# Splitting the last feed-forward's first weight chunk during the output projection, and sharing one token tile's writes differently

## The chip, the cores and the metric

The kernel runs on one core of a Trainium2 chip. The metric is the device time of one execution in microseconds, as the median of several runs. Before the change it is 4000.79 us over 3 runs (3994.6, 4000.79 and 4008.6 us). Engines are named as the profile names them: PE is TensorE, DVE is VectorE, ACT is ScalarE, POOL is GpSimd, SP issues the DMAs.

## What is computed

The reference is a chain of three network blocks over 512 tokens and 1024 channels. Only the end of the third block matters here: a gated merge of two branches, an output projection, a layer norm, a gated feed-forward of 2816 hidden channels and a second layer norm, whose result is the output.

```python
def _layernorm(x, g, b):
    mu = jnp.mean(xf, axis=-1, keepdims=True)
    var = jnp.mean(jnp.square(xf - mu), axis=-1, keepdims=True)
    return ((xf - mu) * lax.rsqrt(var + LN_EPS) * g + b).astype(x.dtype)
...
        x = _layernorm(ALPHA * x + mixed @ w_out[layer], ln1_g[layer], ln1_b[layer])
        ffn = (jax.nn.silu(x @ w_ffn_gate[layer]) * (x @ w_ffn_up[layer])) @ w_ffn_down[layer]
        x = _layernorm(ALPHA * x + ffn, ln2_g[layer], ln2_b[layer])
```

## The kernel before

The program is a list of stages (blocks), one after the other; between two stages all engines meet at a barrier. Inside a stage each engine has its own instruction list, written out by hand, and the lists meet at semaphores. Activations lie with channels on the partitions: `G.x` ("residual") is 8 tiles of 128 channels by 512 tokens.

**Exact products.** A float32 product is made of three passes of a reduced format: each operand is split into a rounded "high" part and the "low" rest, and `exact_product` (L208 to L213) adds high*low, low*high and high*high. So every weight chunk (128 x 4096 numbers, 2 MB) that SP loads into one of two slots of `weight_ring` has to be split before TensorE can use it: one engine copies it into the high part, GpSimd subtracts that from the original for the low part. SP may load chunk n+2 when chunk n has been split (`feed`, L111).

**The merge stage** (`gated_merge`, L4740). GpSimd splits 40 units, a quarter of a chunk each, with a cast (L4036) and a subtraction (L4038). The last 8 units are the output projection. TensorE sums it into PSUM as four token tiles of 128 tokens (j = 0 to 3), in two halves of 512 channels (c = 0, 1), and for each tile it closes the sums and then, one tile behind, turns the normalised rows back (`rows_turned`, L262). After tile 2's turn it waits until tile 0's first half has been written, runs two matmuls of ones to keep busy (`keep_running`, L222) and turns tile 3.

**The layer norm of a token tile** goes round three engines. VectorE measures the two halves (BN_STATS, L271; their total, L273), adds the epsilon (L275), ScalarE takes the root (L287), VectorE inverts it (L277) and multiplies mean and inverse to an offset (L279: a SCALAR_TENSOR_TENSOR on 128 x 1 numbers with two inputs in SBUF). Then ScalarE normalises both halves (L290), TensorE turns them (L262), and the turned tiles, still in PSUM, are scaled and shifted into `G.x`: four instructions on ScalarE for the first 512 channels (`first_columns`, L298) and four on VectorE for the second 512 (`second_columns`, L306). Each engine does the writes of tile j-1 behind its work on tile j. ScalarE so writes tile 2's and tile 3's first halves one after the other at the end, and VectorE tile 2's second half and tile 3's.

**The last feed-forward** (`feed_forward`, called at L4933 as ffn4) starts behind the merge's barrier. Its first up-chunk is in the ring by then, unsplit. ScalarE rounds its first half in 8 pieces (L514), each in front of one tile of the input (L519), with the whole second half (L507) in between; GpSimd subtracts the pieces (L388) and then the second half (L377); VectorE makes the low part of the input (L617). TensorE first runs two matmuls of ones (L222), then the first half piece by piece (48 matmuls), then the second half when GpSimd is done with it. From there on each half is split while TensorE works on an earlier one. The stage ends with the same layer norm, whose writes are followed by eight stores to the output (L368), in order of tile and half.

## Time and profile before

| | us |
|---|---|
| median of 3 runs | 4000.79 |
| the profiled execution | 4000.84 |
| its span, first to last instruction | 3999.1 |
| PE busy | 3857.1 (96%) |
| DVE busy | 2271.8 (57%) |
| POOL busy | 1348.2 (34%) |
| ACT busy | 1339.6 (33%) |

The span is what the rows are timed in: their times count from its start. The last feed-forward runs from about 3620 us to the end, the merge's output projection from about 3574 to 3620 us. A busy share is an average over all stages: it does not say which engine the others wait for in the few microseconds between two stages.

### The profile page before, as it was taken

The numbers are of one execution on the slowest core, as the hardware profiler recorded it, in microseconds if no ns is written. First come the engines' busy times: TensorE is split into PE (matmuls) and PEld (weight loads), VectorE is DVE, ScalarE is ACT, GpSimd is POOL, SyncE is SP. The second block draws the span as 40 slices with busy tenths as digits, with TensorE's granted clock in tenths as the row PEclk, the third lists the DMA queues.
The fourth block names the chain that finished last, engine by engine and source line by source line (L and its number), as shares of the span: only waits on it lengthen the run. The fifth ranks groups of instructions, "written<-read, shape, count | busy, mean of one in ns | idle before, by whom it ended". The sixth has DMA issues, their size and how long they took to land. (4 is left out here: it accounts for less than half of the span.)

```text
span 3999.1 us, 63729 instructions
## 1 busy us (share of the span) xinstructions
PE 3857.1 (96%) x26795; PEld 3057.6 (76%) x26795; DVE 2271.8 (57%) x3322; ACT 1339.6 (33%) x2176; POOL 1348.2 (34%) x554
## 2 busy tenths in 40 slices
PE   8999999999999999988889999999999999999999
PEld 6866788867678887577776788777777777887887
DVE  5756567477667765577884776465551616332023
ACT  3356333243223333444443433322223111204223
POOL 1011444443233441000001444355454343664443
PEclk9999999999999999999999999999999999999999
DMA  5311222232122223431112222222121111322222
GB/s 179 129 62 36 92 105 84 105 113 106 63 80 88 105 88 114 174 138 50 50 41 88 84 95 95 91 85 84 64 84 68 71 67 53 127 84 91 99 93 76
DMA packets 46655, 359.87 MB, mean 90 GB/s; under 512 B 4387, under 2 KB 8867, under 8 KB 27084
## 3 DMA queue, kind: packets, MB, share of 16 engines
q1 hardware_dynamic: 46412, 356.35, 24.7%
q8 instruction: 187, 3.06, 0.3%
q14 instruction: 56, 0.46, 0.0%
HBM read 333.79 MB, written 22.28 MB: 89 GB/s over the span
## 5 line engine op out<-in xcount | busy, mean ns | idle before, releaser
L377 POOL TENSOR_TENSOR ffn_weights_low<-weight_ring,ffn_weights_high 128x2048 fp32r<-128x2048 f32 x128 | 591.4, 4620 | 776.4 <-ACT ffn_weights_high L507 775.6
L211 PE MATMUL banks<-ffn_in_high,ffn_weights_low 128*128 128x512 f32 x1888 | 738.5, 391 | 9.9 <-POOL ffn_weights_low L377 9.0
L212 PE MATMUL banks<-ffn_in_low,ffn_weights_high 128*128 128x512 f32 x1888 | 735.7, 390 | 0.0
L213 PE MATMUL banks<-ffn_in_high,ffn_weights_high 128*128 128x512 f32 x1888 | 735.6, 390 | 0.0
L507 ACT ACTIVATE ffn_weights_high<-weight_ring 128x2048 fp32r<-128x2048 f32 x128 | 245.2, 1915 | 559.1 <-PE banks L213 559.1
L211 PEld LDWEIGHTS banks<-ffn_in_high,ffn_weights_low 128*128 128x128 f32 x1888 | 355.1, 188 | 90.5 <-POOL ffn_weights_low L377 12.0
L212 PEld LDWEIGHTS banks<-ffn_in_low,ffn_weights_high 128*128 128x128 f32 x1888 | 355.1, 188 | 74.1 <-issue 0.7
L213 PEld LDWEIGHTS banks<-ffn_in_high,ffn_weights_high 128*128 128x128 f32 x1888 | 355.1, 188 | 74.0
L652 DVE SCALAR_TENSOR_TENSOR ffn_gate<-ffn_up,columns_sb,ffn_gate 128x511 f32<-128x511 f32 (+1 forms) x132 | 272.9, 2068 | 160.8 <-ACT ffn_value L542 160.8
L4038 POOL TENSOR_TENSOR third_weights_low<-weight_ring,third_weights_high 128x1024 fp32r<-128x1024 f32 x143 | 357.2, 2498 | 11.5
L4036 POOL CAST third_weights_high<-weight_ring 128x1024 fp32r<-128x1024 f32 x143 | 157.3, 1100 | 513.9 <-PE banks L213 485.1
L211 PE MATMUL banks<-third_x_high,third_weights_low 128*128 128x512 f32 x736 | 299.9, 407 | 2.7 <-DVE merge_gate L4898 0.9
L213 PE MATMUL banks<-third_x_high,third_weights_high 128*128 128x512 f32 x736 | 288.3, 392 | 0.0
L212 PE MATMUL banks<-third_x_low,third_weights_high 128*128 128x512 f32 x736 | 287.7, 391 | 0.0
L673 DVE TENSOR_TENSOR ffn_in_low<-ffn_hidden,ffn_in_high 128x512 fp32r<-128x512 f32 x80 | 165.8, 2120 | 141.0 <-ACT ffn_in_high L556 141.0
L3798 POOL TENSOR_TENSOR rwout_weights_low<-weight_ring,rwout_weights_high 128x1024 fp32r<-128x1024 f32 x8 | 18.6, 2380 | 606.7 <-ACT rwout_weights_high L3850 606.7
L211 PEld LDWEIGHTS banks<-third_x_high,third_weights_low 128*128 128x128 f32 x736 | 139.3, 189 | 32.6 <-issue 3.1
L213 PEld LDWEIGHTS banks<-third_x_high,third_weights_high 128*128 128x128 f32 x736 | 138.7, 188 | 30.0
L212 PEld LDWEIGHTS banks<-third_x_low,third_weights_high 128*128 128x128 f32 x736 | 139.4, 189 | 26.7 <-issue 1.0
L545 ACT ACTIVATE ffn_gate<-ffn_gate 128x512 f32<-128x512 f32 x66 | 41.8, 633 | 319.6 <-DVE ffn_gate L652 319.6
L211 PE MATMUL banks<-first_in_high,first_weights_low 128*128 128x512 f32 x336 | 140.0, 417 | 3.5 <-DVE first_in_low L1226 3.5
L665 DVE TENSOR_TENSOR ffn_hidden<-ffn_gate,banks 128x512 f32 (+1 forms) x22 | 15.1, 688 | 217.0 <-ACT ffn_gate L547 217.0
(703 smaller groups left out, 7878.9 us busy)
## 6 DMA issues: line engine op xcount, KB each, us to landing
weight_ring<-weights SPq DMA_DIRECT2D x143, 2048.0 KB, 7.7
scan_in<-rwkv_operands SPq DMA_DIRECT2D x7, 1280.0 KB, 5.7
rwkv_operands<-rwin_staged SPq DMA_DIRECT2D x23, 256.0 KB, 2.2
scan_in<-rwkv_operands SPq DMA_DIRECT2D x8, 512.0 KB, 3.9
bias_tiles<-bias_rows SPq DMA_DIRECT2D x8, 448.0 KB, 8.9
residual<-x SPq DMA_DIRECT2D x4, 512.0 KB, 6.3
hyena_u_x_T<-decay SPq DMA_DIRECT2D x2, 1024.0 KB, 8.1
rwkv_residual<-residual SPq DMA_DIRECT2D x1, 2048.0 KB, 7.2
```

The costliest lines, as they stand in the source:

```text
L211: pe.matmul(out, w[1], x[0], start=start, stop=False, skip_group_check=True)
L212: pe.matmul(out, w[0], x[1], start=False, stop=False, skip_group_check=True)
L213: return pe.matmul(out, w[0], x[0], start=False, stop=stop, skip_group_check=True)
L377: pool.tensor_tensor(parts[1], landed, parts[0].bitcast(F32), ALU.subtract).then_inc(S["split"], 1)
L507: act.activation(parts[0], landed, ACT.Copy).then_inc(S["rounded"], 1)
L545: act.activation(gc[:, h, :], gc[:, h, :], act_func).then_inc(S["activated"], 1)
L652: ins = dve.scalar_tensor_tensor(out=buf[:, h, to], in0=up_scaled[:, h, q, of], scalar=G.col(taps, 8 * t + 4 * q + tap), in1=buf[:, h, to] ...
L665: dve.tensor_tensor(gT[:, t, :], gc[:, h, :], G.banks[:, b + 1, :], ALU.mult).then_inc(S["hidden"], 1)
L673: dve.tensor_tensor(parts[1], gT[:, t, :], parts[0].bitcast(F32), ALU.subtract).then_inc(S["tile_split"], 1)
L3798: pool.tensor_tensor(w_parts[1][:, k, :], landed(k), w_parts[0][:, k, :].bitcast(F32), ALU.subtract).then_inc(S["split"], 1)
L4036: pool.tensor_copy(parts[0], landed).then_inc(S["rounded"], 1)
L4038: pool.tensor_tensor(parts[1], landed, parts[0].bitcast(F32), ALU.subtract).then_inc(S["split"], 1)
```

## The change

The first chunk of ffn4's weights is split before its stage begins. In the merge stage, behind its last input tiles and ahead of the layer norm, ScalarE waits for that chunk to land and copies both halves into new buffers (`ffn4_ahead_high`); GpSimd, behind its 40 units, subtracts both halves into `ffn4_ahead_low`. These buffers lie over the memory of `mlstm_out_T`, which nobody reads any more once the branch's units are used (`used` at 24). ffn4 takes the buffers as its weight buffers and leaves its own out; it raises the semaphores for the pieces at once, and ScalarE there only rounds the input. In all feed-forwards the weight buffers are allocated ahead of the others, so their tiles have other addresses.

The second part: in both layer norms VectorE writes the first half of token tile 2 (`spare_columns`) between tile 2's and tile 3's second halves, and ScalarE no longer does. The stores wait for the new semaphore there.

```diff
@@ -232,7 +232,7 @@
-ROWS = ("row_sum", "row_stats", "row_mean", "row_var", "row_root", "row_inverse", "row_offset", "row_normed", "row_turned", "row_first", "row_second")
+ROWS = ("row_sum", "row_stats", "row_mean", "row_var", "row_root", "row_inverse", "row_offset", "row_normed", "row_turned", "row_first", "row_spare", "row_second")
@@ -299,15 +299,28 @@
+def column_tile(dve, G, name, c, q, j):
...
+    k = JT * c + q
+    return dve.tensor_scalar(G.x[:, k, j * P:(j + 1) * P], row_bank(G, c, j)[:, q * P:(q + 1) * P],
+                             G.col(name + "_g", k), G.col(name + "_b", k), ALU.mult, ALU.add)
...
+def spare_columns(dve, G, R, name, j):
...
+    dve.wait_ge(R["row_turned"], 2 * j + 1)
+    for q in range(JT):
+        column_tile(dve, G, name, 0, q, j).then_inc(R["row_spare"], 1)
...
     for q in range(JT):
-        dve.tensor_scalar(G.x[:, JT + q, j * P:(j + 1) * P], row_bank(G, 1, j)[:, q * P:(q + 1) * P],
-                          G.col(name + "_g", JT + q), G.col(name + "_b", JT + q), ALU.mult, ALU.add).then_inc(R["row_second"], 1)
-def feed_forward(G, name, gain, taps, act_func, shift=0, keep=1.0, norm=None, root=False):
+        column_tile(dve, G, name, 1, q, j).then_inc(R["row_second"], 1)
+def feed_forward(G, name, gain, taps, act_func, shift=0, keep=1.0, norm=None, root=False, ahead=None):
@@ -323,6 +336,8 @@
                   "out_squared", "out_squares_added", "out_sums", "out_mean", "out_root", "out_inverse")
+        w_parts = [G.sb(name + "_weights_" + part, [P, 2, half], F32R, ctx=ctx) for part in ("high", "low")]
+        w_parts = ahead or w_parts
         stats = row_tiles(G, name, ctx) if norm else None
@@ -331,7 +346,6 @@
         vc = G.sb(name + "_value", [P, 2, SEQ], ctx=ctx)
-        w_parts = [G.sb(name + "_weights_" + part, [P, 2, half], F32R, ctx=ctx) for part in ("high", "low")]
         x_parts = [G.sb(name + "_in_" + part, [P, KT, SEQ], F32R, ctx=ctx) for part in ("high", "low")]
@@ -363,8 +377,13 @@
                 for j in range(JT):
-                    for c, columns in enumerate((S["row_first"], S["row_second"])):
-                        sp.wait_ge(columns, JT * (j + 1))
+                    for c in range(2):
+                        if c:
+                            sp.wait_ge(S["row_second"], JT * (j + 1))
+                        elif j == JT - 2:
+                            sp.wait_ge(S["row_spare"], JT)
+                        else:
+                            sp.wait_ge(S["row_first"], JT * min(j + 1, JT - 1))
                         sp.dma_start(G.aps["out"][c * JT * P:(c + 1) * JT * P, j * P:(j + 1) * P].rearrange("(k p) n -> p k n", p=P),
@@ -378,16 +397,21 @@
                 for h in range(2):
-                    if isinstance(i, int) and p == i == h == 0:
+                    if isinstance(i, int) and p == i == 0 and h <= (ahead is not None):
                         continue
...
-            landed, parts = landed_half(0, 0, True)
-            for k in range(KT):
-                pool.wait_ge(S["piece_high"], k + 1)
-                pool.tensor_tensor(parts[1][:, k, :], landed[:, k, :], parts[0][:, k, :].bitcast(F32), ALU.subtract).then_inc(S["piece_split"], 1)
-            pool.wait_ge(S["piece_split"], KT)
-            pool.sem_inc(S["split"], 1)
+            if ahead:
+                pool.sem_inc(S["rounded"], 1)
+                pool.sem_inc(S["piece_split"], KT)
+                pool.sem_inc(S["split"], 2)
+            else:
+                landed, parts = landed_half(0, 0, True)
+                for k in range(KT):
+                    pool.wait_ge(S["piece_high"], k + 1)
+                    pool.tensor_tensor(parts[1][:, k, :], landed[:, k, :], parts[0][:, k, :].bitcast(F32), ALU.subtract).then_inc(S["piece_split"], 1)
+                pool.wait_ge(S["piece_split"], KT)
+                pool.sem_inc(S["split"], 1)
             pairs_from_one(pool, UP_CHUNKS, chunk)
@@ -514,12 +538,13 @@
             for k in range(KT):
-                pieces((k,))
+                if not ahead:
+                    pieces((k,))
                 if gain is None:
...
                     act.activation(x_parts[0][:, k, :], G.x[:, k, :], ACT.Identity, scale=G.col(gain, k)).then_inc(S["x_high"], 1)
-                if k == KT // 2:
+                if k == KT // 2 and not ahead:
                     high(0, 0, 1, True)
@@ -595,7 +620,7 @@
                     rows_normed(act, G, S, stats, rows, j)
-                    if j:
+                    if 0 < j < JT - 1:
                         first_columns(act, G, S, norm, j - 1)
@@ -705,6 +730,7 @@
                         second_columns(dve, G, S, norm, j - 1)
+                spare_columns(dve, G, S, norm, JT - 2)
                 second_columns(dve, G, S, norm, JT - 1)
@@ -4739,7 +4765,7 @@
         S = stage(G, "merge", ctx, "gates_in", "restored", "rounded", "split", "used", "tile_high", "tile_split", "gate_done", "branch_done", "mixed", "kept",
-                  *ROWS)
+                  "next_rounded", "next_split", *ROWS)
@@ -4754,6 +4780,10 @@
+        def next_half(h):
...
+            return G.chunk(units // 4, KT)[:, :, h * 256:(h + 1) * 256], [w[:, h, :].rearrange("p (k n) -> p k n", k=KT) for w in T.next_weights]
@@ -4784,6 +4814,10 @@
                     split_unit(pool, S, column_unit(G, c, n % 4), [w.rearrange("p (k n) -> p k n", k=KT) for w in w_parts(n)], n)
+            for h in range(2):
+                landed, next_parts = next_half(h)
+                pool.wait_ge(S["next_rounded"], h + 1)
+                pool.tensor_tensor(next_parts[1], landed, next_parts[0].bitcast(F32), ALU.subtract).then_inc(S["next_split"], 1)
@@ -4872,9 +4906,14 @@
                 tile_high(tiles + k)
+            act.wait_ge(S["used"], unit_b)
+            G.arrived(act, units // 4 % 2, units // 8)
+            for h in range(2):
+                landed, next_parts = next_half(h)
+                act.activation(next_parts[0], landed, ACT.Copy).then_inc(S["next_rounded"], 1)
             for j in range(JT):
                 rows_normed(act, G, S, stats, rows, j)
-                if j:
+                if 0 < j < JT - 1:
                     first_columns(act, G, S, "ln1", j - 1)
@@ -4911,6 +4950,7 @@
                     second_columns(dve, G, S, "ln1", j - 1)
+            spare_columns(dve, G, S, "ln1", JT - 2)
             second_columns(dve, G, S, "ln1", JT - 1)
@@ -4919,6 +4959,7 @@
         T = Shared()
+        ahead = T.next_weights = G.over("ffn4_ahead_", [P, 2, CHUNK // 2])
         T.haT = G.sb("mlstm_out_T", [P, M_HEADS * MT_, SEQ], ctx=ctx)
@@ -4930,7 +4971,7 @@
             gated_merge(G, T)
-    feed_forward(G, "ffn4", None, None, ACT.Silu, keep=ALPHA, norm="ln2")
+    feed_forward(G, "ffn4", None, None, ACT.Silu, keep=ALPHA, norm="ln2", ahead=ahead)
```

GpSimd's list from the merge's last unit on, before:

```order
L4036 CAST third_x_high<-weight_ring 128x1024
L4038 TENSOR_TENSOR third_x_low<-weight_ring,third_x_high 128x1024
L4740 UNCONDITIONAL_BRANCH
L372 UNCONDITIONAL_BRANCH
L388 TENSOR_TENSOR ffn_weights_low<-weight_ring,ffn_weights_high 128x256 x8
L377 TENSOR_TENSOR ffn_weights_low<-weight_ring,ffn_weights_high 128x2048
```

And with the change (its lines are numbered some 25 to 40 higher; the unconditional branches are the ends of stages):

```order
L4062 CAST third_x_high<-weight_ring 128x1024
L4064 TENSOR_TENSOR third_x_low<-weight_ring,third_x_high 128x1024
L4820 TENSOR_TENSOR ffn_ahead_low<-weight_ring,ffn_ahead_high 128x2048 x2
L4766 UNCONDITIONAL_BRANCH
L391 UNCONDITIONAL_BRANCH
```

Two subtractions of 2048 columns now stand directly behind the last unit, in front of the barrier; eight pieces and one half are gone from behind it.

ScalarE's list from the last input tiles of the projection to the start of ffn4, before:

```order
L4856 ACTIVATE third_x_high<-normed 128x512 x4
L287 ACTIVATE merge_row_inverse<-merge_row_inverse 128x1
L290 ACTIVATE merge_gate<-banks,merge_row_offset,merge_row_inverse 128x512 x2
...
L298 ACTIVATE residual<-banks,columns_sb 128x128 x8
L4740 UNCONDITIONAL_BRANCH
L501 UNCONDITIONAL_BRANCH
L514 ACTIVATE ffn_weights_high<-weight_ring 128x256
L519 ACTIVATE ffn_in_high<-residual 128x512
```

With the change:

```order
L4890 ACTIVATE third_x_high<-normed 128x512 x4
L4913 ACTIVATE ffn_ahead_high<-weight_ring 128x2048 x2
L287 ACTIVATE merge_row_inverse<-merge_row_inverse 128x1
L290 ACTIVATE merge_gate<-banks,merge_row_offset,merge_row_inverse 128x512 x2
...
L298 ACTIVATE residual<-banks,columns_sb 128x128 x4
L4766 UNCONDITIONAL_BRANCH
L525 UNCONDITIONAL_BRANCH
L544 ACTIVATE ffn_in_high<-residual 128x512 x8
```

The two copies stand ahead of the first root; at the end four writes are left of eight, and ffn4 starts with the input tiles alone.

VectorE's list at the end of the merge, before:

```order
L279 SCALAR_TENSOR_TENSOR merge_row_offset<-merge_row_moments,merge_row_inverse 128x1
L306 TENSOR_SCALAR residual<-banks,columns_sb 128x128 x8
L4740 UNCONDITIONAL_BRANCH
L602 UNCONDITIONAL_BRANCH
L617 TENSOR_TENSOR ffn_in_low<-residual,ffn_in_high 128x512 x8
```

With the change:

```order
L279 SCALAR_TENSOR_TENSOR merge_row_offset<-merge_row_moments,merge_row_inverse 128x1
L305 TENSOR_SCALAR residual<-banks,columns_sb 128x128 x12
L4766 UNCONDITIONAL_BRANCH
L627 UNCONDITIONAL_BRANCH
L642 TENSOR_TENSOR ffn_in_low<-residual,ffn_in_high 128x512 x8
```

VectorE has twelve writes behind its last offset where it had eight; the same holds at the end of ffn4.

## Rows read from the trace of the kernel before

**Rows 1.** Timeline, TensorE: start, length, operation, count, idle time before and its releaser.

```profile
3606.00 1.33 PE L262 MATMUL banks<-constants_sb,merge_gate 128*128 128x128 f32 x8
...
3616.41 1.32 PE L262 MATMUL banks<-constants_sb,merge_gate 128*128 128x128 f32 x8 [0.28 <-ACT merge_gate L290]
3620.12 2.42 PE L222 MATMUL banks<-constants_sb 128*128 128x448 f32 x4 [2.39 <-PEq L4740]
3622.02 0.95 PE L211 MATMUL banks<-ffn_in_high,ffn_weights_low 128*128 128x512 f32 x1
...
3634.62 0.50 PE L211 MATMUL banks<-ffn_in_high,ffn_weights_low 128*128 128x512 f32 x1 [0.20 <-POOL ffn_weights_low L377]
```

**Rows 2.** Timeline, ScalarE, the merge's layer norm.

```profile
3605.17 1.45 ACT L290 ACTIVATE merge_gate<-banks,merge_row_offset,merge_row_inverse 128x512 f32<-128x512 f32 x2 [0.42 <-DVE merge_row_offset L279]
...
3616.92 2.90 ACT L298 ACTIVATE residual<-banks,columns_sb 128x128 f32<-128x128 f32 x8
```

**Rows 3.** Timeline, VectorE, the merge's layer norm and ffn4's first input tiles.

```profile
3601.43 0.70 DVE L271 BATCH_NORM_STATS2 merge_row_parts<-banks 128x6 f32<-128x512 f32 x1 [25.34 <-PE banks L213]
3603.38 0.70 DVE L271 BATCH_NORM_STATS2 merge_row_parts<-banks 128x6 f32<-128x512 f32 x1 [1.25 <-PE banks L213]
...
3604.98 0.16 DVE L279 SCALAR_TENSOR_TENSOR merge_row_offset<-merge_row_moments,merge_row_inverse 128x1 f32<-128x1 f32 x1
...
3607.79 1.36 DVE L306 TENSOR_SCALAR residual<-banks,columns_sb 128x128 f32<-128x128 f32 x4
3609.06 0.70 DVE L271 BATCH_NORM_STATS2 merge_row_parts<-banks 128x6 f32<-128x512 f32 x1
...
3615.46 1.36 DVE L306 TENSOR_SCALAR residual<-banks,columns_sb 128x128 f32<-128x128 f32 x4
...
3621.07 5.37 DVE L617 TENSOR_TENSOR ffn_in_low<-residual,ffn_in_high 128x512 fp32r<-128x512 f32 x5 [1.93 <-ACT ffn_in_high L519]
```

**Rows 4.** Timeline, GpSimd, around the barrier.

```profile
3599.24 2.40 POOL L4038 TENSOR_TENSOR third_x_low<-weight_ring,third_x_high 128x1024 fp32r<-128x1024 f32 x1
3620.59 5.30 POOL L388 TENSOR_TENSOR ffn_weights_low<-weight_ring,ffn_weights_high 128x256 fp32r<-128x256 f32 x5 [18.96 <-ACT ffn_weights_high L514]
...
3629.74 4.83 POOL L377 TENSOR_TENSOR ffn_weights_low<-weight_ring,ffn_weights_high 128x2048 fp32r<-128x2048 f32 x1 [0.18 <-POOL ffn_weights_low L388]
```

**Rows 5.** Timeline, VectorE and ScalarE, the last writes of the kernel.

```profile
3990.60 1.36 DVE L306 TENSOR_SCALAR residual<-banks,columns_sb 128x128 f32<-128x128 f32 x4
...
3992.06 2.90 ACT L298 ACTIVATE residual<-banks,columns_sb 128x128 f32<-128x128 f32 x8
```

**Rows 6.** Lines L507 and L377: duration in ns, least, median and most.

```profile
L507 ACT ACTIVATE ffn_weights_high<-weight_ring x128: 1891/1917/1922, 449.8 to 3964.9; 128x2048 fp32r<-128x2048 f32 x128
...
L377 POOL TENSOR_TENSOR ffn_weights_low<-weight_ring,ffn_weights_high x128: 4545/4605/5061, 455.4 to 3966.9; 128x2048 fp32r<-128x2048 f32 x128
```

**Rows 7.** Timeline, SP: the load of ffn4's first chunk.

```profile
3580.28 0.34 SPq L121 DMA_DIRECT2D weight_ring<-weights  x1
```

**Rows 8.** Windows: length, busy time by engine, granted clock, DMA share, GB/s.

```profile
3588.00:3590.00 2.00, 2.00 (x11) 1.65 (x10) 0.00 (x0) 0.00 (x0) 0.78 (x1) 1.00 0.00 0
```

**Rows 9.** Line L1506, a small VectorE operation elsewhere: duration in ns.

```profile
L1506 DVE TENSOR_TENSOR attn_stats<-attn_stats,branch_gates x48: 161/161/1640, 239.9 to 375.5; 128x2 f32<-128x2 f32 x48
```

**Rows 10.** Timeline, GpSimd and VectorE, at one of L1506's long ones.

```profile
243.03 2.37 POOL L1359 TENSOR_TENSOR first_weights_low<-weight_ring,first_weights_high 128x1024 fp32r<-128x1024 f32 x1 [8.39 <-ACT first_weights_high L1443]
...
243.79 1.63 DVE L1506 TENSOR_TENSOR attn_stats<-attn_stats,branch_gates 128x2 f32<-128x2 f32 x1
```

**Rows 11.** Windows, at the start of ffn4, columns as in rows 8.

```profile
3621.10:3624.40 3.30, 3.30 (x8) 2.03 (x7) 3.28 (x4) 3.30 (x9) 3.20 (x4) 0.50 0.00 0
```

**Rows 12.** Timeline, GpSimd and VectorE, VectorE operations with one tensor input.

```profile
2602.38 2.39 POOL L4038 TENSOR_TENSOR third_weights_low<-weight_ring,third_weights_high 128x1024 fp32r<-128x1024 f32 x1
...
2602.41 0.20 DVE L4337 TENSOR_SCALAR gate_small<-gate_small,normed 4x1 f32<-4x1 f32 x1
2602.64 2.20 DVE L4338 TENSOR_SCALAR residual<-residual,normed 4x128 f32<-4x128 f32 x1
```

## The prediction

> **What bounds the kernel now.** TensorE is busy 96% of the span (the table of the profile), so time can only come or go where it waits. I read the waits of the last 400 us first and found TensorE waiting in three places: at the end of the merge, at the start of ffn4 and at the very end. Then I read the timeline of each engine there. In the first place the path is a round of four engines. VectorE's offset (3604.98) releases ScalarE's pass (3605.17), and TensorE's turn of tile 0 starts 0.83 us behind that pass (3606.00) [rows 1, 2, 3]. The last turn ends at 3616.41 + 1.32 = 3617.73, and ScalarE's eight writes end last, at 3616.92 + 2.90 = 3619.82 [rows 1, 2]. Then comes the barrier; TensorE starts ffn4 at 3620.12, 0.30 later, and its first real matmul at 3622.02. Its second half starts at 3634.62, released by GpSimd, which ended at 3629.74 + 4.83 = 3634.57 [rows 1, 4]. At the end of the kernel ScalarE's eight writes (3992.06 + 2.90 = 3994.96) are what the last stores wait for [rows 5].
>
> **The added work.** ScalarE's two copies cost 1.92 us each [rows 6]. The chunk's load is issued at 3580.28 [rows 7], and by 3588 no transfer runs any more, while ScalarE does nothing [rows 8]. So the copies run at about 3588 to 3592, and the next thing ScalarE is wanted for is the first root, shortly before 3604.98. I cost them at nothing; this cover is some 12 us thick. If the chunk came later than about 3600, every us more would delay the first root.
>
> GpSimd's two subtractions are another matter. Its last unit ends at 3599.24 + 2.40 = 3601.64 [rows 4], and only then do they start: 4.61 us each [rows 6], so from about 3601.7 to 3606.3 and from 3606.3 to 3610.9. Nobody waits for their results before 3620. But they run beside the layer norm, during which GpSimd was idle before.
>
> What that does to VectorE is not in the rows of this stage, since there GpSimd was off. Elsewhere it is. L1506, a TENSOR_TENSOR on 128 x 2 numbers whose two inputs lie in SBUF, takes 0.161 us as a rule and up to 1.640 [rows 9]. The long one shown started at 243.79 while GpSimd ran from 243.03 to 245.40, and it ended at 245.42, just behind it [rows 10]. So a VectorE operation with two inputs in SBUF is held until GpSimd's operation is over, however small it is. In the norm's chain that is one operation, the offset L279, on 128 x 1 numbers with both inputs in SBUF. BN_STATS, from PSUM, is not held: it took 0.70 at 3601.43, when GpSimd still ran until 3601.64, and 0.70 at 3603.38, when it was idle [rows 3, 4]. The writes L306 read PSUM too. With the change the chain goes like this, each start worked out from the row named:
>
> Tile 0: the offset is issued at 3604.98 as before, in the middle of GpSimd's first subtraction, and ends at about 3606.35 instead of 3605.14 (+1.2). TensorE's turn of tile 0 starts at 3607.2 instead of 3606.00.
> Tile 1: VectorE needs two BN_STATS, of 0.70 each, and 0.90 more to the offset (3603.38 + 0.70 to 3604.98 [rows 3]): 3606.35 + 2.30 = 3608.65. There GpSimd's second subtraction holds it until 3610.95.
> From here nothing is held, and VectorE has no slack: writes of tile 0 in 1.27 (3607.79 to 3609.06 [rows 3]) to 3612.2, BN_STATS and the rest 2.30 + 0.16 to 3614.7, writes of tile 1 to 3615.9, tile 3's measuring to 3618.4. TensorE's sums are ready for these steps, by my placing: its last turn follows tile 3's offset and is over when VectorE comes to the writes that need it.
>
> **The moved writes.** VectorE now has twelve writes behind the last offset: 2 x 1.27 + 1.36 = 3.9 us, from 3618.4 to 3622.3; ScalarE, with four, is done before. The merge ends at 3622.3 instead of 3619.82: +2.5. Without any holding VectorE would start these writes at 3615.46 [rows 3] and end at 3619.36: -0.45. So the moved writes alone gain 0.45, and the holding costs about 2.95.
>
> **The start of ffn4.** ScalarE starts with the input tile instead of a weight piece, and VectorE's low parts no longer run against GpSimd: five of them took 5.37 us beside five pieces in 5.30 [rows 3, 4]. But TensorE's two matmuls of ones (2.42 [rows 1]) still come first. The first real matmul stood 1.90 behind the start of the stage; it can't come earlier than the ones allow, and the gain lies between 0 and 0.5. I take 0.2, nearer to the row. The wait for GpSimd at 3634.62 is gone: the row gives 0.20 of idle time ahead of a matmul of 0.50 [rows 1]; I take 0.35, between 0.2 and 0.5. What is late next there is TensorE itself, matmul behind matmul.
>
> **TensorE's clock.** It was granted half (1.2 GHz) in 3621.10 to 3624.40 [rows 11]; before that TensorE had been idle from 3617.73 to 3620.12. About 2.4 us of that stretch lay on real matmuls, which cost 1.2. With the change TensorE stalls at other points. If the clock doesn't fall, 1.2 are gained; if the whole stretch of 3.3 us falls on real matmuls, it costs 1.65, 0.45 more than now. I take no difference, since an idle time of some 2 us stays ahead of the barrier's end.
>
> **The end of the kernel.** GpSimd has nothing to do there. VectorE's twelve writes run from 3990.60 to 3994.5 instead of ScalarE's end at 3994.96, and the store of tile 2's first half waits for VectorE at 3990.60 + 2 x 1.27 + 0.1 = 3993.2 instead of ScalarE's fourth write at 3993.5 [rows 5]. I take -0.3, between -0.45 and 0 (the stores may be the limit).
>
> **Other edits.** The new addresses, three more semaphores and an earlier load of the third chunk (SP no longer waits for ffn4's first split) I cost at nothing: no row shows an operation whose time goes by its address, and the load lands in a stretch that is not waited for.
>
> **The sum.** +2.5 - 0.2 - 0.35 - 0.3 = +1.65 us on the profiled execution's 4000.84, which is the median of the runs (4000.79) but for 0.05: 4002.5 us. That is 0.04%, far below the 0.3% (12 us) that a measurement of this kernel can tell from no change; the three runs before lie 14 us apart.
>
> **Rivals.**
> The first: L279 isn't held, or is held once only. For it: no row shows this very operation beside GpSimd. Against it: L1506 is smaller than most and was held all the same. The merge then gains 0.45 instead of losing 2.5: -0.45 - 0.2 - 0.35 - 0.3 = -1.3, so 3999.5, and 3998.3 if the clock doesn't fall.
>
> The second, on the slow side: VectorE is held twice already in tile 0. The add of epsilon (L275), a TENSOR_SCALAR in SBUF, stands some 0.6 ahead of the offset (between 3604.08, where BN_STATS ends, and 3604.98 [rows 3]). If it is held too, it ends at 3606.35, the offset is issued at about 3607.0, inside GpSimd's second subtraction, and ends at 3610.95; tile 1's then at 3610.95 + 2.46 = 3613.4 instead of 3610.95. All that follows is 2.4 later: 4004.9, and 4005.4 with the clock's worse end. It decides if a one-input operation is held at all, since L275 does start inside the first subtraction. The same price stands if GpSimd's second subtraction gets in ahead of the held offset. Rows on both sides: L4338, a TENSOR_SCALAR of 128 columns, started 0.26 behind a GpSimd operation and took 2.20, to its end; L4337, of one column, started 0.03 behind it and took 0.20 [rows 12]. L275 has one column, and the five low parts and five pieces alternated [rows 3, 4], so I think it less likely.
> The Trainium skill (page "SBUF — State Buffer", section "Who interferes with whom") names `tensor_scalar` among the operations that can take the shared ports and then block against GpSimd; by that rule L275 could be held and the time would be this rival's. L4338 agrees with it, L4337 doesn't.
>
> The third: the chunk lands late and ScalarE's wait for it, which stands in order ahead of all roots, becomes the bound. To reach 0.3% it would have to land at about 3612, 24 us later than in this trace [rows 7, 8]. Price: a us for a us from 3600 on; 4013 or more.
>
> **Chances.** Forecast 0.60, first rival 0.18, second 0.17, third 0.02, the remaining 0.03 for what I don't see. All but the third lie within 3998.3 to 4005.4. The median of a few runs scatters by some us more (runs before: 6 below to 8 above their median), so the range is 3995 to 4009. By the same cases: faster by over 0.3% 0.03 (scatter alone), within it 0.92, slower 0.05 (scatter and the third rival).
>
> **What would show it.** In the new profile L279's rows for tiles 0 and 1 take about 1.4 and 2.3 us instead of 0.16, each ending with one of GpSimd's subtractions; VectorE's last write in the merge ends about 2.5 us later; TensorE idles longer ahead of the turns of tiles 0 and 1. In ffn4 TensorE's first 96 matmuls run without a wait for GpSimd. The last write of the kernel comes from VectorE. If L279 takes 0.16, the first rival holds; if L275 is long, the second. A merge that ends early together with a time of over 4010 would show a cost that this text doesn't know.

## The result, and the profile after

The changed kernel takes 4017.11 us (median of 14 runs, 4012.36 to 4025.75), the kernel before 4007.91 in 14 runs (3994.6 to 4013.57); the ratio is 1.0029, with a 95% interval of 1.0022 to 1.0036. The change made the kernel slower, by 0.2 to 0.3%: 9.2 us by the medians, 11.6 by the ratio. I had predicted 4002.5 us and a range of 3995 to 4009. Part of that miss is the base: the first three runs of before had a median of 4000.79, the fourteen have 4007.91, 7.1 us more. The rest is the change, which I had at +1.65.

The profiled execution of the changed kernel has a span of 4024.1 us, of before 3999.1. Their 25 us don't all belong to the change. I lined up the matmuls of the two traces and looked where the difference of their start times grows. Up to the end of ffn2 it stays below 1 us. Between ffn2's last and ffn3's first split matmul, where the RWKV scan lies and nothing was changed, before takes 665.6 us and the changed kernel 678.5; over the 14 traces of this study that stretch lies between 665.6 and 678.5, without order. It is scatter, and it is about half of the 25. So I compare one stretch of each trace: from the first statistics of the merge to the end of the span. It takes 397.7 us before and 407.4 after: +9.66, which fits the medians.

Where in that stretch it goes is read from two views. First the merge, VectorE's timeline in the changed kernel, from tile 0's statistics to the last writes; it answers to [rows 3]:

```profile
3616.68 0.70 DVE L271 BATCH_NORM_STATS2 merge_row_parts<-banks 128x6 f32<-128x512 f32 x1 [25.32 <-PE banks L213]
...
3619.63 0.15 DVE L275 TENSOR_SCALAR merge_row_inverse<-merge_row_moments 128x1 f32<-128x1 f32 x1
...
3620.25 1.22 DVE L279 SCALAR_TENSOR_TENSOR merge_row_offset<-merge_row_moments,merge_row_inverse 128x1 f32<-128x1 f32 x1
...
3623.57 2.42 DVE L279 SCALAR_TENSOR_TENSOR merge_row_offset<-merge_row_moments,merge_row_inverse 128x1 f32<-128x1 f32 x1
...
3627.20 1.28 DVE L271 BATCH_NORM_STATS2 merge_row_parts<-banks 128x6 f32<-128x512 f32 x2
...
3629.38 0.16 DVE L279 SCALAR_TENSOR_TENSOR merge_row_offset<-merge_row_moments,merge_row_inverse 128x1 f32<-128x1 f32 x1
3629.45 1.36 DVE L305 TENSOR_SCALAR residual<-banks,columns_sb 128x128 f32<-128x128 f32 x4
...
3633.00 3.91 DVE L305 TENSOR_SCALAR residual<-banks,columns_sb 128x128 f32<-128x128 f32 x12
```

GpSimd's and ScalarE's timelines of the same time, answering to [rows 4] and [rows 2]:

```profile
3614.51 2.38 POOL L4064 TENSOR_TENSOR third_x_low<-weight_ring,third_x_high 128x1024 fp32r<-128x1024 f32 x1
3616.85 9.14 POOL L4820 TENSOR_TENSOR ffn_ahead_low<-weight_ring,ffn_ahead_high 128x2048 fp32r<-128x2048 f32 x2
```

```profile
3603.25 3.72 ACT L4913 ACTIVATE ffn_ahead_high<-weight_ring 128x2048 fp32r<-128x2048 f32 x2 [14.64 <-DMA weight_ring<-weights]
3619.82 0.20 ACT L287 ACTIVATE merge_row_inverse<-merge_row_inverse 128x1 f32<-128x1 f32 x1 [12.85 <-DVE merge_row_inverse L275]
3621.51 1.45 ACT L290 ACTIVATE merge_gate<-banks,merge_row_offset,merge_row_inverse 128x512 f32<-128x512 f32 x2 [1.49 <-DVE merge_row_offset L279]
...
3626.03 1.45 ACT L290 ACTIVATE merge_gate<-banks,merge_row_offset,merge_row_inverse 128x512 f32<-128x512 f32 x2 [2.69 <-DVE merge_row_offset L279]
```

The copies are done at 3606.97, twelve us before ScalarE is wanted again. (The merge stands 15.25 us later in this trace than in before's; with that taken off they run from 3588.0 to 3591.7, as predicted.) GpSimd's two subtractions follow its last unit, and the offset is held until each is over: 1.22 and 2.42 us in tiles 0 and 1, 0.16 in the others. L275 is not held (0.15). The last write ends at 3636.91, 20.23 us behind the first statistics, where before needed 18.39: +1.84.

Then the start of ffn4, TensorE's timeline, answering to [rows 1], and the window that answers to [rows 11]:

```profile
3637.23 1.74 PE L222 MATMUL banks<-constants_sb 128*128 128x448 f32 x4 [1.96 <-PEq L4766]
3638.71 0.49 PE L211 MATMUL banks<-ffn_in_high,ffn_ahead_low 128*128 128x512 f32 x1
```

```profile
3638.20:3641.50 3.30, 3.30 (x15) 2.37 (x14) 3.30 (x7) 3.28 (x7) 0.00 (x0) 1.00 0.94 318
```

There is no stretch at half clock and no wait for GpSimd any more. At this point the changed kernel has won back most of the merge's loss. The loss of time is in none of the waits; it is in the matmuls themselves. These are 200 us of ffn4's first phase in before and in the changed kernel (columns as in [rows 8]; the number behind PE's busy time counts its matmuls):

```profile
3638.00:3838.00 200.00, 200.00 (x884) 165.62 (x883) 13.06 (x19) 47.58 (x45) 86.02 (x19) 1.00 0.27 101
```

```profile
3656.00:3856.00 200.00, 200.00 (x859) 160.67 (x858) 12.40 (x18) 47.29 (x44) 81.67 (x19) 1.00 0.26 94
```

Both are busy throughout, at full clock, but the same time holds 25 matmuls fewer. A split product is one exact product, three matmuls. From its start to the next one's start it is 680 ns in before, 226.7 per matmul, as in ffn1 to ffn3 of both kernels. In the changed kernel's ffn4 it is 700 ns, 233.3 per matmul, in both phases: the first works on the up-chunks and the second on the down-chunks. Each of these matmuls holds 128 x 128 numbers of one operand (the stationary one) and streams 512 columns of the other (the moving one). In ffn4's first phase the weights' parts are stationary and the input tiles move; in its second the weights' parts move. Ffn4 has 1584 of them (the expectations below say 1576); from the 200th to the last it takes 328.47 us instead of 319.49.

The end, VectorE and ScalarE, answering to [rows 5]: the last write is now VectorE's, 6.01 us behind the start of the last matmul instead of 6.46.

```profile
4015.81 3.91 DVE L305 TENSOR_SCALAR residual<-banks,columns_sb 128x128 f32<-128x128 f32 x12
```

```profile
4017.45 1.50 ACT L298 ACTIVATE residual<-banks,columns_sb 128x128 f32<-128x128 f32 x4
```

The whole ledger, in us, worked out from the start and end times of the traces (a matmul counts by its start); "low" says whether the trace shows the clock at half in ffn4's first microseconds. The kernels in the lower part are those of the experiments.

```
kernel            statistics   to ffn4's    to the   to the   to the   to the   sum     low
                  to last      first        100th    200th    last     end
                  write        matmul       matmul   matmul   matmul
before            18.39        2.20         24.32    22.67    319.49   10.65    397.72  yes
after             20.23        1.80         23.20    23.33    328.47   10.35    407.38  no
e4_order_only     18.39        2.20         24.65    23.34    328.47   10.66    407.70  yes
e6_stats_last     20.23        1.80         22.58    22.67    319.53   10.35    397.15  no
e7_offset_act     18.12        1.80         22.57    22.66    319.67   10.13    394.95  no
e9_one_input      18.00        1.84         24.16    22.67    319.56   10.39    396.62  yes
e10_spare_only    17.95        2.21         24.29    22.67    319.51   10.35    396.98  no
e11_pad480        20.22        1.80         22.55    22.67    319.51   10.35    397.10  no
e12_ahead_only    20.66        1.79         24.18    22.67    319.53   10.67    399.50  yes
```

### The profile page after: what moved, and what is told of

It reads as the page before. It is cut to its first block and busy times, and to the rows that moved or that the text cites. A ratio compares the mean times of both kernels' runs of the same rounds, so it can differ in the third digit from the quotient of the medians.

```text
span 4024.1 us, 63718 instructions
## 1 busy us (share of the span) xinstructions
PE 3879.3 (96%) x26795; PEld 3068.0 (76%) x26795; DVE 2275.1 (57%) x3330; ACT 1336.9 (33%) x2161; POOL 1345.8 (33%) x547
## 5 line engine op out<-in xcount | busy, mean ns | idle before, releaser
L396 POOL TENSOR_TENSOR ffn_weights_low<-weight_ring,ffn_weights_high 128x2048 fp32r<-128x2048 f32 x96 | 443.7, 4622 | 582.0 <-ACT ffn_weights_high L531 581.5
L211 PE MATMUL banks<-ffn_in_high,ffn_weights_low 128*128 128x512 f32 x1536 | 600.7, 391 | 9.7 <-POOL ffn_weights_low L396 8.8
L212 PE MATMUL banks<-ffn_in_low,ffn_weights_high 128*128 128x512 f32 x1536 | 598.3, 390 | 0.0
L213 PE MATMUL banks<-ffn_in_high,ffn_weights_high 128*128 128x512 f32 x1536 | 598.2, 389 | 0.0
L211 PEld LDWEIGHTS banks<-ffn_in_high,ffn_weights_low 128*128 128x128 f32 x1536 | 288.6, 188 | 75.6 <-POOL ffn_weights_low L396 11.3
L213 PEld LDWEIGHTS banks<-ffn_in_high,ffn_weights_high 128*128 128x128 f32 x1536 | 288.7, 188 | 60.5
L212 PEld LDWEIGHTS banks<-ffn_in_low,ffn_weights_high 128*128 128x128 f32 x1536 | 288.7, 188 | 59.8 <-issue 0.7
L531 ACT ACTIVATE ffn_weights_high<-weight_ring 128x2048 fp32r<-128x2048 f32 x96 | 183.8, 1915 | 309.3 <-PE banks L213 309.3
L396 POOL TENSOR_TENSOR ffn_ahead_low<-weight_ring,ffn_ahead_high 128x2048 fp32r<-128x2048 f32 x31 | 143.4, 4627 | 226.9 <-ACT ffn_ahead_high L531 226.9
L531 ACT ACTIVATE ffn_ahead_high<-weight_ring 128x2048 fp32r<-128x2048 f32 x31 | 59.4, 1917 | 261.6 <-PE banks L213 261.6
```

The lines of the kernel that those rows point to most:

```text
L211: pe.matmul(out, w[1], x[0], start=start, stop=False, skip_group_check=True)
L212: pe.matmul(out, w[0], x[1], start=False, stop=False, skip_group_check=True)
L213: return pe.matmul(out, w[0], x[0], start=False, stop=stop, skip_group_check=True)
L396: pool.tensor_tensor(parts[1], landed, parts[0].bitcast(F32), ALU.subtract).then_inc(S["split"], 1)
L531: act.activation(parts[0], landed, ACT.Copy).then_inc(S["rounded"], 1)
```

## The experiments

Nothing in ffn4's matmuls was changed but where their operands lie. The program's allocation gives the places. A partition's weight parts start at byte 152960 in before and at 89184 in the changed kernel; ffn4's input tiles start at 185728 in both. (Ffn4's own weight buffers, which the change no longer uses, are still allocated, over the same bytes as the new ones, so nothing behind them moved up.) In ffn1 to ffn3 of the changed kernel the weight parts also start at 89184, the input tiles at 185440, and their matmuls kept 226.7 ns. The 288 bytes between these two input addresses are ffn4's row statistics, which the other three don't have. With the weights now ahead of the statistics, they came between weights and inputs. So theory A was that the start of the one operand against the start of the other, modulo some small power of two, sets the pace.

**One change of 32 bytes, and its multiples.** The edit (64 and 96 bytes: 16 and 24 in place of 8; 480 bytes, run later: 120):

```
         stats = row_tiles(G, name, ctx) if norm else None
+        pad = G.sb(name + "_pad", [P, 8], ctx=ctx) if norm else None
```

> The changed kernel with 32 unused bytes behind ffn4's statistics, so that its input, hidden and early tiles all lie 32 bytes further on; the weight parts stay where the change put them. Theory A (alignment): in the changed kernel ffn4's weight parts begin at 32 modulo 64 bytes of a partition and its input tiles at 0 modulo 64, and every other split product of both kernels has both alike. If that costs the 6.7 ns by which each of ffn4's 1576 split matmuls is longer (233.3 instead of 226.7 ns from start to start), the pad brings 226.7 ns back and the time falls by about 1576 x 6.7 = 10.5 us, to about 4007 where the changed kernel has 4017: same as before within 3 us. Rival B (the place): the weight parts' distance from the input tiles, or their place in memory, costs it; 32 bytes change neither, and the matmuls stay at 233.3 ns, the time at 4017. Rival C (the clock): ffn4's matmuls are slower because the clock was not lowered at the start of ffn4 in that execution; nothing changes but by chance. The sum of my prediction for the rest (about +1.7 against before) is tested by the same run: under A 4009.5.

> The same with 64 bytes in place of 32: ffn4's input tiles lie at 0 modulo 64 again, but at another distance from the weight parts. Theory A: 233.3 ns per matmul as in the changed kernel, about 4017 us (one execution, 4012 to 4026). Theory B, if it is one particular distance that costs: 226.7 ns.

> The changed kernel with 96 unused bytes behind ffn4's statistics: input, hidden and early tiles and weight parts then all begin at 96 modulo 128 bytes, but 128 apart modulo 256. With 32 bytes of pad (64 apart modulo 128) the matmuls of ffn4's first phase took 229.0 ns and those of the second still 233.8, with 64 (96 apart) 233.3 and 234.3, without one (32 apart) 233.3 and 233.5. Theory A128 (both have to be alike modulo 128): 226.7 ns in both phases, and 10.5 us less in ffn4 than the changed kernel. Theory A256 (modulo 256 or more): at least one phase stays above 228 ns.

> The changed kernel with 480 unused bytes behind ffn4's statistics: weight parts and input tiles are then alike modulo 256 and 256 apart modulo 512. 96 bytes of pad (128 apart modulo 256) gave 232.4 ns in both phases, and statistics at the end (alike modulo 2048) 226.7. If alike modulo 256 is enough: 226.7 ns; if it takes 512: above 228 ns.

With 32 bytes: 4016.56 us where before had 4010.84 on that chip, ratio 1.0016 (1.0006 to 1.0025). The matmuls of ffn4's first phase went to 228.9 ns, those of the second stayed at 233.3 (a mean over 300 matmuls; the expectation of e5 gives 233.8 for them). Theory B, which had no change, falls; theory A in the form I wrote down (modulo 64) falls too, since both were then at 32 modulo 64. With 64: 4026.57 us in one run, 233.3 and 234.3 ns. With 96: 4021.08, 232.4 in both, so alike modulo 128 isn't enough. With 480: 4006.33 and 226.7 in both. Windows of 200 us of e1, e5 and e11, in that order:

```profile
3650.00:3850.00 200.00, 200.00 (x875) 164.12 (x874) 12.37 (x18) 47.31 (x44) 83.79 (x19) 1.00 0.26 94
```

```profile
3650.00:3850.00 200.00, 200.00 (x862) 162.16 (x861) 12.38 (x18) 47.98 (x46) 82.56 (x19) 1.00 0.26 94
```

```profile
3650.00:3850.00 200.00, 200.00 (x884) 165.58 (x884) 12.40 (x18) 49.90 (x47) 83.44 (x19) 1.00 0.26 94
```

The counts go 875, 862, 884 with nothing but the pad changed. In the traces of e1, e2 and e5 ffn1 to ffn3, which have no pad, kept 226.7 ns. The combinations of the whole study, those of e3, e4 and e6 (below) among them; the difference is that of the inputs' start less that of the weights':

```
kernel and stage        weights at  inputs at  difference     ns per matmul
                                               modulo 256     1st   2nd phase
before, ffn1 to ffn3    152672      185440     0              226.7 226.7
before, ffn4            152960      185728     0              226.7 226.7
after, ffn1 to ffn3      89184      185440     0              226.7 226.7
e6, ffn4                 89184      185440     0              226.7 226.7
e11, ffn4                89184      186208     0              226.7 226.7
after and e4, ffn4       89184      185728     32             233.3 233.3
e3, ffn1 to ffn3        152672      185472     32             233.3 233.3
e3, ffn4                152960      185760     32             233.3 233.3
e1, ffn4                 89184      185760     64             228.9 233.3
e2, ffn4                 89184      185792     96             233.3 234.3
e5, ffn4                 89184      185824     128            232.4 232.4
```

Input tiles at 185728 are fast with one place of the weights and slow with the other, and weights at 89184 are fast with some inputs and slow with others. It is the pair that counts. A difference of a whole number of 256 bytes gave full pace in all five cases. Another one cost 1.0 to 3.4% in all six. That 256 is enough, and 512 not needed, rests on e11 alone: the other four fast differences are multiples of 512.

The table also holds a reading that would explain why the two phases of e1 and e2 differ. In ffn4's second phase the operands have changed places. Counted as the moving operand's start less the stationary one's, e1 has 64 in the first phase and 192 in the second, e2 has 96 and 160, and e5, with the same pace in both, has 128 in both. So counted, the paces are 233.3 ns at 32, 228.9 at 64, 233.3 at 96, 232.4 at 128, 234.3 at 160, 233.3 at 192 and 233.3 at 224. No run tests this reading by itself.

**The same in the kernel before, in all four feed-forwards.**

```
+        pad = G.sb(name + "_pad", [P, 8], ctx=ctx)
         x_parts = [G.sb(name + "_in_" + part, [P, KT, SEQ], F32R, ctx=ctx) for part in ("high", "low")]
```

> The kernel before with 32 unused bytes between weight parts and input tiles in all four feed-forwards, and nothing else: weight parts at 32 modulo 64 and input tiles at 0 in ffn1 to ffn3, the other way round in ffn4. Theory A: all four go to 233.3 ns per split matmul, 4 x 1576 x 6.7 ns = +42 us, about 4050; if only one way round costs, +31 or +10.5. Theory B: no change, 4008. Theory C: no change.

4046.57 us against 4010.84, ratio 1.0080 (1.0065 to 1.0095). All four feed-forwards show 233.3 ns. A window of 200 us in ffn1, of before and of this kernel:

```profile
500.00:700.00 200.00, 200.00 (x881) 165.51 (x880) 141.82 (x132) 74.83 (x77) 86.28 (x19) 1.00 0.26 94
```

```profile
500.00:700.00 200.00, 200.00 (x855) 160.57 (x855) 139.91 (x131) 72.40 (x75) 83.40 (x18) 1.00 0.26 94
```

From first to last split matmul ffn2 takes 372.48 us instead of 363.03, and the four together 38.2 us more. I had 42, by 6.7 ns on each; the loops absorb a part of it in waits that they have anyway (ffn2's pauses between matmuls add up to 3.1 us where before has 4.0). Thirty-two unused bytes cost this kernel 0.8%.

**The order of allocation alone.**

```
+        w_parts = [G.sb(name + "_weights_" + part, [P, 2, half], F32R, ctx=ctx) for part in ("high", "low")]
         stats = row_tiles(G, name, ctx) if norm else None
...
-        w_parts = [G.sb(name + "_weights_" + part, [P, 2, half], F32R, ctx=ctx) for part in ("high", "low")]
```

> The kernel before with one edit of the change alone: the weight parts are allocated first in all feed-forwards. No chunk is split ahead and no write moved. Theory A: ffn1 to ffn3 as before (all at 32 modulo 64), ffn4 at 233.3 ns: +10 us, about 4018, and the barrier's 10 us wait of GpSimd's pieces as before. Theory C (the clock's low stretch at the start of ffn4 makes the difference): it still falls here, so ffn4 keeps 226.7 ns and the time 4008.

4020.73 against 4010.84, ratio 1.0023 (1.0014 to 1.0032), and 233.3 ns in ffn4 alone. In the ledger it stands 9.98 us above before, all of it from ffn4's matmuls. This trace has the low clock at ffn4's start, so theory C falls as well: the change's loss is there without its chunk, without its writes and with the clock as before.

**The change with its operands put right.** The statistics are allocated last:

```
-        stats = row_tiles(G, name, ctx) if norm else None
...
         early = [G.sb(name + "_early_" + part, [P, EARLY, SEQ], F32R, ctx=ctx) for part in ("high", "low")]
+        stats = row_tiles(G, name, ctx) if norm else None
```

> The changed kernel with ffn4's statistics allocated last, behind the early tiles, so that its input, hidden and early tiles begin where those of ffn1 to ffn3 do (a whole number of 2048 bytes from the weight parts). Theory A: 226.7 ns per split matmul in both phases of ffn4, and what is left of the change by the trace of the changed kernel: merge's last write +1.84, first matmuls of ffn4 (no low clock, no wait for GpSimd) about -1.4, tail -0.45: together 0.0, so the time of before within 2 us (about 4011 by the runs shared with the last experiments, 4008 by the earlier ones). Rival B (the place in memory): the matmuls stay at 233 ns and the time at about 4017 to 4020. Rival by my own prediction's sum: +1.7 against before, since it gave the low clock nothing.

4008.97 against 4005.83, ratio 1.0009 (1.0000 to 1.0018), clearly below the changed kernel's 1.0029 (1.0022 to 1.0036), each against the runs of before beside it. Full pace in ffn4, as these 200 us of its first phase show:

```profile
3650.00:3850.00 200.00, 200.00 (x884) 165.59 (x883) 15.93 (x20) 48.28 (x46) 86.98 (x19) 1.00 0.26 94
```

The ledger's sum is 397.15: -0.57 against before and -10.23 against the changed kernel. That the median came out 3 us above before, where the ledger has -0.57, is at the edge of the interval; I put it down to the scan, but no run settles it.

**The offset without two SBUF inputs.** In e7 ScalarE forms it from a mean that VectorE has negated (first piece); in e8 and e9 VectorE does, with the inverse root as a per-partition scalar (second piece). Both take out the operation of two inputs, and all three kernels have e6's allocation (e9 is e8's kernel, run again and timed):

```
-    dve.scalar_tensor_tensor(out=offset[:, j:j + 1], in0=moments[:, j, 0:1], scalar=-1.0, in1=inverse[:, j:j + 1],
-                             op0=ALU.mult, op1=ALU.mult).then_inc(R["row_offset"], 1)
```

```
+    dve.tensor_scalar(offset[:, j:j + 1], moments[:, j, 0:1], -1.0, None, ALU.mult).then_inc(R["row_negated"], 1)
...
+    act.activation(offset[:, j:j + 1], offset[:, j:j + 1], ACT.Identity, scale=inverse[:, j:j + 1]).then_inc(R["row_offset"], 1)
```

```
+    dve.tensor_scalar(offset[:, j:j + 1], moments[:, j, 0:1], inverse[:, j:j + 1], -1.0, ALU.mult, ALU.mult).then_inc(R["row_offset"], 1)
```

> The kernel of e6 with the layer norms' offset on ScalarE: VectorE negates the mean right behind its variance step, and ScalarE multiplies it by the inverse root just ahead of its two normalizing operations, so that no VectorE operation with two SBUF inputs stands between the root and the normalized rows. Theory H (GpSimd's subtractions hold VectorE's two-input offset, 1.22 and 2.42 us against 0.16 in the changed kernel): the holds of token tiles 0 and 1 go, merge's last write ends about 2 us earlier than in e6 against its own start, and ffn4 starts as much earlier; the tail changes by -0.2 to +0.2. Time 2 us below e6. Rival: VectorE's other small operations (add, negate, reciprocal) are held in the offset's place, and nothing is won.

> The kernel of e6 with the offset still on VectorE, but written with one tensor input and the inverse root as a per-partition scalar operand. If two tensor inputs are what GpSimd's subtraction holds up, the offset takes 0.16 us in all four token tiles of merge; if a per-partition scalar from SBUF is held as well, it takes 1.2 and 2.4 us in tiles 0 and 1 as in the changed kernel.

> The kernel with ffn4's statistics allocated last and the offset written with one tensor input, now timed. By one trace of it, merge's layer norm and ffn4 together take 1.1 us less than in the kernel before (396.6 against 397.7 us from the first statistics of merge to the end), with a low clock at the start of ffn4 in that execution; without one 2.4 less. Expected 0.9997 to 0.9993 of before; since the executions scatter by 10 us in the scan, the interval will hold 1. Rival: the low clock goes as in the changed kernel, and the stretch is 395.2 us.

GpSimd's and VectorE's timelines in e9:

```profile
3612.75 9.17 POOL L4819 TENSOR_TENSOR ffn_ahead_low<-weight_ring,ffn_ahead_high 128x2048 fp32r<-128x2048 f32 x2
```

```profile
3616.16 0.21 DVE L279 TENSOR_SCALAR merge_row_offset<-merge_row_moments,merge_row_inverse 128x1 f32<-128x1 f32 x1
3618.90 0.21 DVE L279 TENSOR_SCALAR merge_row_offset<-merge_row_moments,merge_row_inverse 128x1 f32<-128x1 f32 x1
```

GpSimd runs from 3612.75 to 3621.92, and both offsets take 0.21 us in the middle of it. The merge's last write comes at 18.00 us (e8 and e9) and 18.12 (e7) instead of 20.23: -2.1 to -2.2, as expected. The rival, that another small operation takes the hold over, falls: in e7 VectorE's negation took 0.14 us beside GpSimd, its reciprocal 0.16. The Trainium skill (page "SBUF — State Buffer", section "SBUF: two separate sides") names a VectorE operation with two SBUF inputs as one that locks against GpSimd for a whole instruction; the rows agree, in e9 by the missing hold. The times: e7 4004.55 against 4005.83, ratio 1.0000 (0.9991 to 1.0009); e8 4003.35 in one run; e9 4006.63 against 4008.52, ratio 0.9998 (0.9990 to 1.0007). They beat the changed kernel, but most of that is e6's allocation, which they share, and their intervals overlap e6's: the offset's own gain is read from the traces alone. Against before the ledger has -1.1 (e9, with the low clock) and -2.8 (e7, without), and no timing here can tell that from nothing.

**The parts apart.** In e10 the kernel before has the moved writes alone, in both layer norms; e12 is e6 without them. For the merge, e10's edit, which e12 takes back:

```
-                if j:
+                if 0 < j < JT - 1:
                     first_columns(act, G, S, "ln1", j - 1)
...
+            spare_columns(dve, G, S, "ln1", JT - 2)
             second_columns(dve, G, S, "ln1", JT - 1)
```

> The kernel before with the moved writes alone: VectorE writes the first channels of the last but one token tile in both layer norms; no chunk ahead, allocation as before. By my prediction merge's last write comes 0.45 us earlier after merge's first statistics (18.39 us in before, so 17.94) and the last write of the kernel 0.45 earlier after the last matmul (6.46, so 6.01); from the first statistics to the end 397.7 - 0.9 = 396.8 us if the end follows. Rival: the GpSimd wait of ffn4's pieces hides the first one, since GpSimd starts at the barrier: still earlier, as the barrier is; or the stores bind the end and 0.3 of the second is kept, as in the changed kernel (10.35 against 10.65 to the end).

> The kernel with ffn4's statistics allocated last, without the moved writes: the chunk ahead alone. The offset is held 1.2 and 2.4 us as in the changed kernel; merge's last write then comes 0.45 us later than with the moved writes, at 20.23 + 0.45 = 20.7 us after the first statistics, the tail is that of before (6.46), and 1576 matmuls at 226.7 ns stay. From the first statistics to the end 397.15 + 0.75 = 397.9 us, if the clock is not lowered at the start of ffn4; 399.2 if it is.

The moved writes do what I had worked out, to 0.01 us: 17.95 to the merge's last write and 6.02 from the last matmul to the last write; 0.30 of the second reaches the end. The sum is 396.98, -0.74; the one timed run took 4004.00 us. The chunk alone (4007.67 in one run) costs: the last write comes at 20.66, and with the low clock in this trace the sum is 399.50, +1.78 (expected 399.2 for that case). E10 also shows something I had not seen in before. Its clock isn't lowered at ffn4's start, and yet its first 100 matmuls take 24.29 us, as in before. Its TensorE and GpSimd there:

```profile
3638.08 0.50 PE L211 MATMUL banks<-ffn_in_high,ffn_weights_low 128*128 128x512 f32 x1 [1.47 <-POOL ffn_weights_low L395]
```

```profile
3633.21 4.82 POOL L395 TENSOR_TENSOR ffn_weights_low<-weight_ring,ffn_weights_high 128x2048 fp32r<-128x2048 f32 x1 [0.18 <-POOL ffn_weights_low L406]
```

At full clock TensorE reaches the second half sooner and waits 1.47 us for it. In before that wait was 0.20 [rows 1], because the low clock [rows 11] lay over it. The low clock by itself can be seen where the chunk was split ahead: the first 100 matmuls take 24.0 to 24.2 us with it (e8, e9, e12) and 22.6 without (e6, e7, e11): some 1.5 us.

## Why the prediction was wrong

The failed step is the one on the other edits: "The new addresses ... I cost at nothing: no row shows an operation whose time goes by its address". The addresses cost 10.23 us (the changed kernel against e6), more than all the rest together. The reason given was no reason. No row of before could show such an operation, since in before weights and inputs are a whole number of 256 bytes apart in all feed-forwards; by the program's allocation that holds for the two operands of every fp32r matmul of before, and in the changed kernel for all but ffn4's. A cost that the rows can't show has to get bounds. I gave it zero and no width, and so the range ended at 4009. My own last sentence came near it ("A merge that ends early together with a time of over 4010 would show a cost that this text doesn't know"), but here the merge ended late, by 1.84 us; what I didn't see had three in a hundred. The base is a separate fault: the three runs of before put it 7.1 us under the median of fourteen, and on that median my sum would have been 4009.6.

The other terms, against the ledger:

- The held offset: mechanism right. I had 1.4 and 2.3 us, the rows show 1.22 and 2.42, each with GpSimd beside it. The first rival (not held) falls; so does the second, as L275 took 0.15. The Trainium skill's rule beside that rival (page "SBUF — State Buffer", section "Who interferes with whom") lets `tensor_scalar` block against GpSimd when its operands meet further conditions; at 128 x 1 these traces show no hold, neither in L275 (0.15 us) nor in e9's offset (0.21).
- Merge's end: +2.5 predicted, +1.84 measured. I gave VectorE 2.46 us for each later tile from its first statistics to its writes; the rows show 2.25 (3627.20 to 3629.45), and this counts twice. The second hold also ended 9.31 us behind the first statistics, where I had 9.52. The sign and the cause stand.
- The moved writes: -0.45 predicted, 17.95 against 18.39 measured alone.
- Start of ffn4: -0.2 predicted for the first matmul, -0.40 measured. For GpSimd's wait and the clock together I had -0.35 and 0. The traces have -0.2 (e9) where the clock is low and -1.74 (e6) where it isn't. My bound of 1.2 for the clock was near; what I missed is that the low clock and the wait for GpSimd lay one over the other, so removing either alone gains next to nothing. My reason for no difference, that an idle time of some 2 us stays, didn't decide it: with 1.96 us of it the clock stayed full in the changed kernel, with 1.95 it fell in e9.
- End of the kernel: -0.3 predicted, -0.30 measured.
- The chunk's arrival (third rival): the copies ran at 3603.25 to 3606.97 and held nobody up, as predicted.
- The sum without the addresses: +1.65 predicted, -0.57 measured in e6 without the low clock; with it, by the 1.5 us that the low clock costs the first 100 matmuls, about +0.9.

So the rest of the change, as far as these runs tell, is worth nothing either way. Its early chunk gains 0.4 us at ffn4's first matmul and 1.7 at best in the first hundred, and pays 2.3 in the merge, nearly all of it through the offset (e12's last write at 20.66 against 18.39).

## What to carry to other kernels

An edit that only moves a buffer is not free by default. Before it is costed at nothing, write down the start addresses of the two operands of each long row of matmuls, and compare them with a stage that is known to be fast; here the 288 bytes stood in the allocation for anyone to subtract. When two delays end near each other, as the low clock and GpSimd's piece did, look at what each costs with the other gone. And in a kernel that scatters by up to 13 us in one stage, compare stretches of the traces that begin behind it.

## What the runs showed of the hardware

- For these fp32r matmuls with 128 x 128 weights and 512 columns, the pace from start to start depended on how weight and input addresses stand to each other: 226.7 ns where they differ by a multiple of 256 bytes, 228.9 to 234.3 at 32, 64, 96 and 128. Both phases show it, and in ffn4's second the weights' parts are the moving operand. Why, and whether other matmul forms do the same, no run here shows.
- A VectorE operation on 128 x 1 numbers with two SBUF inputs was held 1.2 to 2.4 us by GpSimd; the same product with one input and a per-partition scalar took 0.21 beside it. In before a TENSOR_SCALAR of 128 columns was held [rows 12], so the small size may matter.
- Of 14 traces 7 show the clock at half in ffn4's first microseconds (3.4 us, in e5 6.8) and 7 don't, among them kernels that differ by a pad alone. TensorE's idle time ahead of the stage was 2.39 us in four of them (before, e3, e4, e12), and all four had the low clock; of the ten with 1.73 to 1.96 us three had it (e5, e8, e9). What decides it stays open.
